# Where the operands of the products lie in SBUF: after the constant tables, or ahead of them

## What is computed

```python
x = x + 0.5 * _swiglu(_rmsnorm(x, g[0]), ffn_w_in[li, 0], ffn_w_out[li, 0])   # layer li = 0, 1
h = _rmsnorm(x, g[1])                       # li = 0: _hgrn2_mixer(h), li = 1: _mla_mixer(h)
...
x = x + 0.5 * _swiglu(_rmsnorm(x, g[2]), ffn_w_in[li, 1], ffn_w_out[li, 1])
x = x + gate * (p[li] @ ple_w_in[li])       # gate = sigmoid(_rmsnorm(x, g[3]) @ ple_w_gate[li])
...
# second model: even_mixer, conv_ffn, odd_mixer, conv_ffn, each on a normed x and added to x
```

## Time and profile before

| | us |
|---|---|
| median of 3 runs | 1856.1 (1855.09 to 1857.44) |
| profiled execution, its own time | 1859.32 |
| profiled execution, span | 1857.5 |
| TensorE busy in the span | 1790.9 |

### The profile page before, as it was taken

The page is one execution under the profiler, slowest core; times in us unless marked ns, Lnnn a source line. Parts: engine busy times, 40 slices in busy tenths (PEclk is TensorE's granted clock), DMA queues, the critical chain, the costliest instruction groups (busy, mean ns, idle before and its releaser), DMA issues.

```text
span 1857.5 us, 36683 instructions
## 1 busy us (share of the span) xinstructions
PE 1790.9 (96%) x14492; PEld 1759.8 (95%) x14492; DVE 1189.8 (64%) x1764; ACT 957.1 (52%) x1097; POOL 351.7 (19%) x280
## 2 busy tenths in 40 slices
PE   7999989989999999999999999989899999989999
PEld 7999989979999989998998999988899999989998
DVE  6555679986554665546545655565487776567776
ACT  5444667774434753445335444474365545655453
POOL 2000400030004600016564000467400011020001
PEclk9999989999999999999999999999899999999999
DMA  6556323335555355544343555433345453345452
GB/s 215 216 184 238 116 93 118 111 114 203 181 181 174 133 188 182 182 156 141 118 147 118 200 181 188 176 136 137 114 159 190 171 192 124 127 159 181 181 203 91
DMA packets 45168, 298.25 MB, mean 161 GB/s; under 512 B 5024, under 2 KB 5408, under 8 KB 15920
## 3 DMA queue, kind: packets, MB, share of 16 engines
q1 hardware_dynamic: 45104, 297.38, 45.2%
HBM read 296.31 MB, written 1.05 MB: 160 GB/s over the span
## 4 chain that ended last, share of the span: by engine, by line
PE 81%; DVE 10%; ACT 5%; issue 3%; DMA 1%; POOL 0%; SPq 0%; ACTq 0%; DVEq 0%
PE wk L380 15%; PE wk L381 15%; PE wk L382 15%; PE acc L380 8%; PE acc L381 8%; PE acc L382 8%; DVE sumsq L678 1%; PE wk L1032 1%; DVE x_lo L457 1%; PE wk L391 1%; PE wk L390 1%; PE wk L392 1%; ACT w_hi L326 1%; DVE x L422 1%; ACT tmp L619 1%
## 5 line engine op out<-in xcount | busy, mean ns | idle before, releaser
L326 ACT ACTIVATE w_hi<-raw 128x2048 fp32r<-128x2048 f32 (+5 forms) x300 | 532.5, 1783 | 432.2 <-PE wk L382 358.3
L381 PE MATMUL wk<-x_lo,w_hi 128*128 128x256 f32 x2560 | 727.1, 284 | 0.0
L380 PE MATMUL wk<-x_hi,w_hi 128*128 128x256 f32 x2208 | 632.0, 286 | 17.8 <-DVE x_lo L457 11.3
L2602 POOL TENSOR_TENSOR w_lo<-raw,w_hi 128x512 fp32r<-128x512 f32 (+1 forms) x274 | 351.0, 1316 | 1490.9 <-ACT w_hi L326 1490.8
L382 PE MATMUL wk<-x_hi,w_lo 128*128 128x256 f32 x2208 | 627.0, 284 | 0.0
L352 DVE TENSOR_TENSOR w_lo<-raw,w_hi 128x2048 fp32r<-128x2048 f32 (+2 forms) x218 | 484.1, 2222 | 170.2 <-ACT w_hi L326 170.2
L381 PEld LDWEIGHTS wk<-x_lo,w_hi 128*128 128x128 f32 x2560 | 492.1, 192 | 0.4
L380 PEld LDWEIGHTS wk<-x_hi,w_hi 128*128 128x128 f32 x2208 | 425.1, 193 | 21.2 <-DVE x_lo L457 12.5
L382 PEld LDWEIGHTS wk<-x_hi,w_lo 128*128 128x128 f32 x2208 | 424.9, 192 | 0.0
L380 PE MATMUL acc<-h_hi,w_hi 128*128 128x256 f32 x1376 | 392.2, 285 | 16.3 <-DVE h_lo L2191 4.8
L381 PE MATMUL acc<-h_lo,w_hi 128*128 128x256 f32 x1376 | 387.7, 282 | 0.0
(11 more groups left out here) (323 smaller groups left out, 2146.5 us busy)
## 6 DMA issues: line engine op xcount, KB each, us to landing
raw<-w_ffn_loop SPq DMA_DIRECT2D x120, 1024.0 KB, 4.8
raw<-w_conv_loop SPq DMA_DIRECT2D x60, 1024.0 KB, 4.8
raw<-w_mla_loop SPq DMA_DIRECT2D x18, 768.0 KB, 4.3
raw<-w_hgrn_loop SPq DMA_DIRECT2D x10, 896.0 KB, 4.5
raw<-w_ple_gate SPq DMA_DIRECT2D x8, 1024.0 KB, 4.8
raw<-w_odd_loop SPq DMA_DIRECT2D x10, 768.0 KB, 4.2
raw<-w_even_loop SPq DMA_DIRECT2D x6, 1024.0 KB, 4.8
raw<-w_odd_proj SPq DMA_DIRECT2D x6, 1024.0 KB, 4.8
```

The source lines that it names most:

```text
L326: nc.scalar.activation(w_hi[slot][:, 0:n], raw[slot][:, 0:n], ACT.Copy).then_inc(S("hi_ready"), 1)
L380: nc.tensor.matmul(dst, hi, a_hi, start=start, stop=False, skip_group_check=True)
L381: nc.tensor.matmul(dst, hi, a_lo, start=False, stop=False, skip_group_check=True)
L2602: last = nc.gpsimd.tensor_tensor(w_lo[slot][:, a:b], raw[slot][:, a:b], w_hi[slot][:, a:b].bitcast(F32), ALU.subtract)
```

## The change

The change only reorders allocations: no instruction, loop, wait or transfer is added, removed or moved. `w_hi`, `w_lo`, `x_hi`, `x_lo`, `c_hi`, `c_lo`, `q_both` and `x_lo_2` are allocated behind `h_val`, that is behind `par`, `cst` and the small tables. `raw` and `x` stay ahead.

```diff
         raw = [sb(f"raw{s}", [P, SLOT_TILES * P]) for s in range(SLOTS)]
-        w_hi = [sb(f"w_hi{s}", [P, SLOT_TILES * P], F32R) for s in range(SLOTS)]
-        w_lo = [sb(f"w_lo{s}", [P, SLOT_TILES * P], F32R) for s in range(SLOTS)]
         x = sb("x", [P, KD, SEQ])
-        x_hi = sb("x_hi", [P, KD, SEQ], F32R)
-        x_lo = sb("x_lo", [P, KD, SEQ], F32R)
         par = sb("par", [P, N_PARAMS])
         cst = sb("cst", [P, N_CONSTS])
...
         h_val = sb("h_val", [P, 2, SEQ])
-
+        x_hi = sb("x_hi", [P, KD, SEQ], F32R)
+        x_lo = sb("x_lo", [P, KD, SEQ], F32R)
+        c_hi = sb("c_hi", [P, 2, SEQ], F32R)
+        c_lo = sb("c_lo", [P, 2, SEQ], F32R)
+        q_both = sb("q_both", [P, KD, SEQ], F32R)
+        x_lo_2 = sb("x_lo_2", [P, KD, SEQ], F32R)
+        w_hi = [sb(f"w_hi{s}", [P, SLOT_TILES * P], F32R) for s in range(SLOTS)]
+        w_lo = [sb(f"w_lo{s}", [P, SLOT_TILES * P], F32R) for s in range(SLOTS)]
         tmp = sb("tmp", [P, 8, SEQ])
...
         lat = tmp[:, 0:4, :]
-        c_hi = sb("c_hi", [P, 2, SEQ], F32R)
-        c_lo = sb("c_lo", [P, 2, SEQ], F32R)
-        q_both = sb("q_both", [P, KD, SEQ], F32R)
         q_hi, q_lo = q_both[:, 0:4, :], q_both[:, 4:8, :]
-        x_lo_2 = sb("x_lo_2", [P, KD, SEQ], F32R)
         k_rope = sb("k_rope", [P, SEQ])
```

## The result

The change made the kernel slower by a third of a per cent: 1861.5 us (median of 7 runs, 1857.5 to 1864.2) against 1856.1 for the kernel before (7 runs, 1853.7 to 1857.4), ratio 1.0031 with a 95% interval of 1.0018 to 1.0044. The forecast was 1865.

A forecast was written before the change was run, and what follows sets the result against it. The prediction took the kernel to be bound by TensorE's pace from product to product. Its terms, 6.6 + 2.2 + 0.3 = 9.1 us on the median of 1856.1, gave 1865.2, taken as 1865, range 1838 to 1868.

The forecast's parts named there:

- The distance sets the pace: All products: moving operand's place relative to the stationary one within 512 bytes decides; distance 0 gives 120.0 ns.
- The 48 products with h: Sign in a group of ffn0: these would take 5.76 us after the change instead of 5.66.
- the 96 with x: Sign in a group of ffn0: these would still take 11.52 us; with rival 1, 11.32.
- the stretches at 113: Sign in mla and even: three stretches of 48 products with h at 113.3 ns vanish if distance 0 allows only the slow rhythm.
- the prediction's own case: Whole kernel slower by 9 us, its own range 1862 to 1867, chance 0.41.
- Products with x, q and c: Moving x, `q_both`, `x_lo_2` and c: stay at 120.0 ns at distance 0, cost 0.
- Products with h: Go from 117.9 to 120.0 ns: 6.6 us in ffn and conv stages, up to 2.7 in the mixers, counted as 2.2.
- Stationary c: 96 instructions with c stationary lose 2.7 ns each, 0.3 us.
- The factor of 0.81 for the mixers: TensorE's chain share, applied to the mixers' (1.0 + 1.7) us because TensorE sometimes waits there: 2.2 us.
- Rival 1: Moving operand's place alone decides; x and q products speed up, 16.5 us fewer, about 1840; chance 0.27, including a half effect.
- Rival 2: Place does not matter, h is faster by its order through `acc`; no pace changes, 1856; chance 0.27.
- Rival 3: Distance 0 is worse than thought where it is new; 1870 and more; chance 0.05.

The follow-up runs named there:

- h alone: Kernel before with only `h_hi` and `h_lo` moved, by padding, to distance 0 from the weights: 1861.8 us against 1853.0, ratio 1.0045.
- the sweep: Separate kernel streaming 96 products per distance, 0 to 480 bytes in steps of 32, computing none of the model: 120.0 ns at 0, 117.8 at 64, 113.3 at 192.
- The control: Kernel before with 256 more bytes ahead of `h_hi`, every distance within 256 bytes unchanged: 1857.2 us against 1856.2, ratio 1.0007.
- the copy of the weights: Streams over weights copied 64 bytes further: moving places 64, 128, 0 and 192 gave 120.0, 117.8, 117.8 and 120.0 ns.
- the streams that alternate in `wk`: Streams alternating between two halves of `wk` instead of walking through `acc`: 120.0, 117.8, 118.6 and 113.3 ns at distances 0, 64, 128 and 192.
- distance 192: Changed kernel with 320 bytes of padding ahead of `w_hi`, all moving activations 192 bytes from the weights: 1830.7 us against 1855.1 for the kernel before, ratio 0.9859.
- a true 48: Changed kernel with all operands carved from one tensor, each 48 bytes behind a multiple of 64, distance 0: 1847.3 us, ratio 0.9961 to the kernel before.
- The distance of 112: Changed kernel with operands carved from one tensor, activations at 112 and weights at 0 within 256 bytes: 1805.5 us against 1853.6 for the kernel before, ratio 0.9735.

## Why the prediction was right, and where it was too narrow

**The mechanism.** "The distance sets the pace" held for the case at hand. Distance 0 gave 120.0 to every product, h alone is the whole effect, and the sweep shows 120.0 and 117.8 without any other engine. The 48 products with h took the 5.76 us that the prediction named, the 96 with x the 11.52, and the stretches at 113 vanished. These signs bear the mechanism out. That 1861.5 lies in the range of 1838 to 1868 says little by itself, since the range was made to hold the rivals' times too; and it lies just below 1862 to 1867, the range of the prediction's own case.

**The terms.** Products with x, q and c: 0 expected, -0.6 and +0.35 us found. Products with h: 6.6 + 2.7 = 9.3 us before anything is absorbed, 9.1 found in the intervals. Stationary c and the other token tiles: 0.3 expected, 0.2 found. The total was 9.1 expected and 5.4 found (1861.5 - 1856.1). 9.1 us would be a ratio of 1.0049, just above the changed kernel's interval (to 1.0044), so a part of the paced 9.0 probably does not arrive; the change with h alone cost 8.8, and its interval (1.0031 to 1.006) holds 1.0049. The control shows that the stretches at the lower clock vary by more than this from one execution to the next at unchanged paces, and h alone had 353 intervals at 213 ns against the 346 of before: that distance 0 shortens them is not borne out.

The waits show a pattern: they sum to 108.9 and 109.3 us in the two kernels with h at distance 0, and to 113.2 and 114.3 in the two with h at 64. So some 4 us of slower products may be absorbed in waits for other engines. With one profile of each kernel this is indicated and not shown, and the missing 3 to 4 us stay open. The factor of 0.81 for the mixers, worth 0.5 us, is too small for these runs to judge.

**Rival 1** (the moving operand's place alone decides, 1840) is refuted by the changed kernel, in which x came to h's old place and stayed at 120.0, and by the copy of the weights in the first sweep. **Rival 2** (the place doesn't matter, h is faster by its order through `acc`) is refuted by h alone, ratio 1.0045, and by the streams that alternate in `wk`. The rule beside it, that of the Trainium skill (SBUF — State Buffer, Who interferes with whom), that TensorE's two read ports are independent and that it never waits on anyone, would leave the pace alone; it doesn't agree with these runs, in which the pace of the same instruction goes from 113.3 to 123.3 ns with no other engine at work. **Rival 3** (distance 0 worse than 120) did not come.

**What was too narrow.** The prediction called the pace a rhythm and saw that "one set of addresses can have two paces", then priced the distance as if it were the only thing. For this change that did no harm, since 120.0 was the only pace ever seen at distance 0 and a multiple of 32. Carried one step beyond this change, it fails: at distance 192 the streams' 113.3 ns did not carry over to the whole kernel, and 24 of 75 us came. The distance, the common place (at distance 0, within 32 bytes) and the products just ahead choose the rhythm together. The distance of 112 was worth more because it settled in one rhythm behind every neighbour tried.

The rounding of sizes also mattered more than the prediction thought: it said that its own rule would give the same time without rounding. At a true 48 with distance 0 the kernel takes 1847.3 us, against 1855.1 for the kernel as it was before. A kernel before without rounding was not run.

**Open.** Why two streams of reads fall into these rhythms, and why 112 found the fast one behind every neighbour tried, no run here shows. Nor does one show what chooses between the rhythms when a stage begins. Only the behaviour is measured.

## What to carry to other kernels

When TensorE is busy nearly all the time, read its pace from start to start and not from the mean of a group: 120.0 and 117.8 ns hid behind 284 and 285. If the paces of equal instructions differ, print the addresses of both operands within 256 bytes and measure a stream of 100 products at each distance, and again behind others, before the layout is chosen. A place that is fast behind every neighbour is worth more than one that is fast alone, and part of what a faster TensorE gains comes back as waits for other engines: here 17.2 of 67.3 us.

## What was unexpected

- A product of 256 columns in fp32r, with its own weight load, takes 113.3 to 123.3 ns at 2.4 GHz by the operands' places and the products just ahead, with a period of 256 bytes of distance. At 1.2 GHz it is 213 ns for h and x alike.
- Two rhythms, 117.8 and 113.3 ns, at one set of addresses. In the streams the products just ahead choose; in a whole kernel the pace changed behind a pause and then held, once over 1344 products.
- At distance 0, two operands 16 or 48 behind a multiple of 64 run at 118.4 ns and those at 0 or 32 at 120.0.
- Allocations alone moved this kernel from 1861.5 to 1805.5 us, with the same instructions in the same order.
